# The first norm of a two-block transformer kernel: raw turn, normed tiles in PSUM, two units side by side

## The reference

```
h = x * rsqrt(mean(x * x, -1) + eps) * norm_mix          # x: 512 tokens x 1024
proj = h @ dn_w_in                                       # 1024 x (4 * 1024 + 16)
qkv = silu(depthwise_conv(proj[..., :3072], conv_w))     # 4 taps along the tokens
beta = sigmoid(b); g = -exp(a_log) * softplus(a + dt_bias)   # a, b: last 16 columns
k = l2_normalize(k)                                      # per head of 128
```

## Time and profile before

| | us |
|---|---|
| median of 3 runs | 1165.15 |
| lowest, highest | 1163.28, 1165.2 |
| the profiled execution | 1164.43 |
| its span (first to last instruction) | 1162.6 |
| TensorE busy | 1114.5 (96%) |
| TensorE weight loads | 908.2 (78%) |
| VectorE, GpSimd, ScalarE busy | 581.8, 486.7, 469.7 |

### The profile page before, as it was taken

One profiled execution on the slowest core, in us unless ns is written; L12 is line 12 of the kernel. 1 busy time (PEld: TensorE's weight loads), 2 busy tenths in 40 slices (PEclk: granted clock), 3 DMA queues, 4 the chain that ended last, 5 costly groups with the idle time before them and its releaser, 6 DMA issues. The chain is left out here.

```text
span 1162.6 us, 16417 instructions
## 1 busy us (share of the span) xinstructions
PE 1114.5 (96%) x5820; PEld 908.2 (78%) x5820; DVE 581.8 (50%) x1246; ACT 469.7 (40%) x1002; POOL 486.7 (42%) x280
## 2 busy tenths in 40 slices
PE   5999999999999899999999999899999999999995
PEld 4888888888887778888888888777788888656674
DVE  3576846666547564522122126445653654344465
ACT  5544345555534432431331333333333434343343
POOL 4575422323226584774674575454121211132220
PEclk8999999999999899999999999899999999999997
DMA  7453441221204453443443444422112010001001
GB/s 219 114 129 98 129 107 46 64 56 38 55 19 132 129 161 117 122 147 123 129 144 117 136 145 119 113 55 73 37 37 64 28 38 28 10 9 37 21 35 73
DMA packets 161175, 100.36 MB, mean 86 GB/s; under 512 B 24065, under 2 KB 154445, under 8 KB 160077
## 3 DMA queue, kind: packets, MB, share of 16 engines
q1 hardware_dynamic: 160812, 98.80, 29.5%
q10 hardware_dynamic: 288, 0.59, 0.2%
HBM read 96.21 MB, written 3.16 MB: 85 GB/s over the span
## 5 line engine op out<-in xcount | busy, mean ns | idle before, releaser
L1161 POOL TENSOR_TENSOR wlo<-stage,whi 128x1024 fp32r<-128x1024 f32 (+1 forms) x105 | 272.3, 2598 | 248.0 <-ACT whi L705 247.7
L2095 PE MATMUL ps<-hhi,whi 128*128 128x512 f32 (+1 forms) x744 | 307.3, 413 | 8.3 <-DVE hlo L1750 2.4
L2095 PE MATMUL ps<-hlo,whi 128*128 128x512 f32 (+1 forms) x744 | 303.0, 407 | 0.0
L2095 PE MATMUL ps<-hhi,wlo 128*128 128x512 f32 (+1 forms) x744 | 296.5, 398 | 0.0
L2095 PEld LDWEIGHTS ps<-hhi,whi 128*128 128x128 f32 (+1 forms) x744 | 141.9, 191 | 50.7 <-issue 17.1
L705 ACT ACTIVATE whi<-stage 128x1024 fp32r<-128x1024 f32 x104 | 109.5, 1055 | 130.3 <-PE ps L2095 99.6
L2095 PEld LDWEIGHTS ps<-hhi,wlo 128*128 128x128 f32 (+1 forms) x744 | 141.6, 190 | 25.6
L2095 PEld LDWEIGHTS ps<-hlo,whi 128*128 128x128 f32 (+1 forms) x744 | 142.0, 191 | 24.1 <-issue 2.8
L1250 POOL TENSOR_TENSOR wlo<-stage,whi 128x1024 fp32r<-128x1024 f32 (+3 forms) x40 | 73.4, 1838 | 197.7 <-ACT whi L991 197.7
L2095 PE MATMUL ps<-ahi,whi 128*128 128x512 f32 x320 | 127.7, 399 | 4.4 <-POOL alo L1238 2.8
L1067 ACT ACTIVATE prob<-ps,aneg 128x128 f32<-128x128 f32 (+1 forms) x96 | 50.6, 527 | 199.7 <-issue 102.1
(11 more groups left out here) (365 smaller groups left out, 1792.6 us busy)
## 6 DMA issues: line engine op xcount, KB each, us to landing
stage<-dn_w_in SPq DMA_DIRECT2D x32, 512.0 KB, 4.0
stage<-mlp_w_up SPq DMA_DIRECT2D x32, 512.0 KB, 4.5
stage<-mlp_w_down SPq DMA_DIRECT2D x32, 512.0 KB, 4.6
mod_w<-ada_w SPq DMA_DIRECT2D x8, 1536.0 KB, 6.4
stage<-w_in SPq DMA_DIRECT2D x17, 512.0 KB, 3.6
gcrow<-gc_rows SPq DMA_DIRECT2D x16, 256.0 KB, 3.5
stage<-dn_w_out SPq DMA_DIRECT2D x8, 512.0 KB, 3.6
stage<-w_in SPq DMA_DIRECT2D x9, 256.0 KB, 3.0
```

The costliest lines, as they stand in the source:

```text
L1161: pool.tensor_tensor(wlo[:, slot, 0:ks, 0:cols], stage[:, slot, 0:ks, 0:cols], whi[:, slot, 0:ks, 0:cols], ALU.subtract).then_inc(s["w_lo" ...
L2095: mm = pe.matmul(bank, w[:, slot, k - ks[0], 0:width], x[:, k], start=(i == 0), stop=(i == len(todo) - 1))
```

## The change

1. The first norm. x is transposed raw, a token tile at a time, as soon as it lands (`raw_turn(c)`, eight blocks into two banks), and VectorE copies it to `xT`. ScalarE still squares (now into `hlo` as waste) and takes roots, and then makes a diagonal matrix of the inverse roots (`root_diagonal`); a product of ones with it (`root_row`) lays the inverse roots as a row over all partitions in bank 7. `norm_mix` comes as 8 rows of 128 and is turned to a column per tile. VectorE makes each normed tile in one of five PSUM banks (`normed`), ScalarE copies its high part, VectorE subtracts the low part (`normed_low`). Nine products of the identity with itself, whose result is not used, follow the last root row.
2. Units 0 and 1 run side by side: for each tile as its `hhi` comes the high weights of both, and the low weights (those of unit 1 three tiles later); then the transposes of the vector rows; then all products with `hlo`, unit 1 four tiles behind.
3. ScalarE's first tap of `k0` and VectorE's three taps come ahead of the gates' last steps, ScalarE's tanh for `k0` ahead of the three exponentials, and the squares of `k0` ahead of the copy to `gct`. TensorE's sums for the gates stand after 15 products of `k1`, the transpose of `gcs` after 21. The raw transposes between products and their copies are gone.

The diff, cut to its core (left out: semaphore names, the tensors `diag`, `ones0`, `nmix`, `gcol`, which take the place of `gbc` and `xr`, and plain removals that the text above names):

```diff
+            def root_diagonal(c):
+                act.wait_ge(s["x_inv"], c + 1)
+                act.activation(diag[:, c, :], K["ident"], ACT.Copy, scale=rtok[:, 1, c:c + 1]).then_inc(s["x_dg"], 1)
+
+            act.wait_ge(s["ident_in"], 16)
             for c in range(CH):
                 act.wait_ge(x_in[c], 16)
-                act.activation(ps[:, 6:8, :], xn[:, c, :].rearrange("p (b n) -> p b n", b=2), ACT.Square,
+                act.activation(hlo[:, KT - 2:KT, :], xn[:, c, :].rearrange("p (b n) -> p b n", b=2), ACT.Square,
                                scale=float(D) ** -0.5, accum_out=msq[:, c:c + 1]).then_inc(s["x_sq"], 1)
                 act.wait_ge(s["x_sq"], c + 1)
                 act.activation(rtok[:, 0, c:c + 1], msq[:, c:c + 1], ACT.Sqrt, bias=epsc[:, :]).then_inc(s["x_rms"], 1)
-            for f in range(2 * CH):
-                c, half = f // 2, f % 2
-                act.wait_ge(s["h_tr"], f + 1)
-                act.activation(hhi[:, half * 4:half * 4 + 4, c * P:(c + 1) * P],
-                               ps[:, 2 + f % 4, :].rearrange("p (k i) -> p k i", k=4), ACT.Copy).then_inc(s["h_hi"], 1)
-            for n in range(1, 4):
+                if c:
+                    root_diagonal(c - 1)
+            root_diagonal(CH - 1)
+            split_hi(1, 1)
+            for k in range(KT):
+                act.wait_ge(s["x_f"], k + 1)
+                act.activation(hhi[:, k], hf0(k), ACT.Copy).then_inc(s["h_hi"], 1)
+            for n in range(2, 4):
                 split_hi(n, n)
...
 
             act.wait_ge(s["gate_in"], 32)
             act.activation(dtb[:, 1, :], dtb[:, 1, :], ACT.Exp).then_inc(s["gate_act"], 1)
+            act.wait_ge(s["vec_col"], 2)
+            tap0("k0")
             act.wait_ge(s["ba_col"], 1)
             act.activation(gtmp[:, 0], batok[:, :, 0:H], ACT.Tanh, scale=0.5).then_inc(s["gate_act"], 1)
             act.wait_ge(s["gate_dve"], 2)
@@ -766,25 +782,19 @@
             act.wait_ge(s["gate_act"], 3)
             act.activation(gtmp[:, 2], gtmp[:, 2], ACT.Ln, bias=1.0).then_inc(s["gate_act"], 1)
             split_hi(RING, 0)
-            act.wait_ge(s["vec_col"], 2)
-            tap0("k0")
+            conv_tanh("k0")
             act.wait_ge(s["gate_ps"], 1)
             for n in range(3):
                 act.activation(gates[:, :, 1 + n, :].rearrange("p h c -> p c h"),
                                ps[:, 4, 32 * n:32 * n + 32].rearrange("p (c h) -> p c h", h=H),
                                ACT.Exp).then_inc(s["gate_ready"], 1)
             act.activation(cact[:, :], V["c_2"], ACT.Tanh, scale=0.5).then_inc(s["mod_c"], 1)
-            conv_tanh("k0")
+            k_squares(0)
             act.wait_ge(s["gct_ps"], 1)
             act.activation(gct[0:H * CH, :], ps[0:H * CH, 4, P:2 * P], ACT.Copy).then_inc(s["gct_ready"], 1)
             next_split("k0")
...
+            pool.memset(ones0[:, :], 1.0).then_inc(s["ones_set"], 1)
...
+            dve.wait_ge(s["nm_tr"], 1)
+            dve.tensor_copy(gcol[:, :], ps[:, 0, 0:KT]).then_inc(s["nm_col"], 1)
+            for c in range(CH):
                 dve.wait_ge(s["x_rms"], c + 1)
                 dve.reciprocal(rtok[:, 1, c:c + 1], rtok[:, 0, c:c + 1]).then_inc(s["x_inv"], 1)
-                dve.wait_ge(s["x_inv"], c + 1)
-                dve.scalar_tensor_tensor(out=xr[:, c % 2], in0=xn[:, c, :], scalar=rtok[:, 1, c:c + 1], in1=gbc[:, :],
-                                         op0=ALU.mult, op1=ALU.mult).then_inc(s["x_nrm"], 1)
-
-            def h_low(f):
-                c, half = f // 2, f % 2
-                cut = (slice(0, P), slice(half * 4, half * 4 + 4), slice(c * P, (c + 1) * P))
-                dve.wait_ge(s["h_hi"], f + 1)
-                dve.tensor_tensor(hlo[cut], ps[:, 2 + f % 4, :].rearrange("p (k i) -> p k i", k=4), hhi[cut], ALU.subtract)\
-                    .then_inc(s["h_lo"], 1)
-
-            dve.wait_ge(s["gbc_in"], 16)
-            x_normed(0)
-            x_normed(1)
-            for c in range(CH):
-                for half in range(2):
-                    h_low(c * 2 + half)
-                if c < 2:
-                    x_normed(c + 2)
+                b = 2 + c % 2 * 2
+                dve.wait_ge(s["xtr"], c + 1)
+                dve.tensor_copy(xT[:, :, c * P:(c + 1) * P], ps[:, b:b + 2, :].rearrange("p b (k i) -> p (b k) i", k=KT // 2))\
+                    .then_inc(s["xev"], 1)
+            dve.wait_ge(s["nm_col"], 1)
+            dve.wait_ge(s["xev"], CH)
+            dve.wait_ge(s["rs_ps"], CH)
+
+            def normed(k):
+                if k >= 5:
+                    dve.wait_ge(s["h_lo"], k - 4)
+                dve.scalar_tensor_tensor(out=hf0(k), in0=xT[:, k], scalar=gcol[:, k:k + 1], in1=ps[:, 7, :],
+                                         op0=ALU.mult, op1=ALU.mult).then_inc(s["x_f"], 1)
+
+            def normed_low(k):
+                dve.wait_ge(s["h_hi"], k + 1)
+                dve.tensor_tensor(hlo[:, k], hf0(k), hhi[:, k], ALU.subtract).then_inc(s["h_lo"], 1)
+
+            for k in range(5):
+                normed(k)
+            for k in range(5, KT):
+                normed_low(k - 5)
+                normed(k)
+            for k in range(KT - 5, KT):
+                normed_low(k)
...
+            taps("k0")
...
+            silu2("k0", kT[:, 0])
...
+            pe.wait_ge(s["nm_in"], 16)
+            pe.transpose(ps[:, 0, 0:KT], nmix[0:KT, :], ident[0:KT, 0:KT]).then_inc(s["nm_tr"], 1)
+
+            def raw_turn(c):
+                pe.wait_ge(x_in[c], 16)
+                if c >= 2:
+                    pe.wait_ge(s["xev"], c - 1)
+                for k in range(KT):
+                    mm = pe.transpose(ps[:, 2 + c % 2 * 2 + k // 4, k % 4 * P:(k % 4 + 1) * P], xn[:, c, k * P:(k + 1) * P], ident)
                 mm.then_inc(s["xtr"], 1)
+
+            def root_row(c):
+                pe.wait_ge(s["x_dg"], c + 1)
+                pe.matmul(ps[:, 7, c * P:(c + 1) * P], ones0[:, :], diag[:, c, :], start=True, stop=True).then_inc(s["rs_ps"], 1)
+
+            pe.wait_ge(s["ones_set"], 1)
+            raw_turn(0)
+            for c in range(1, CH):
+                raw_turn(c)
+                root_row(c - 1)
+            root_row(CH - 1)
+            for _ in range(9):
+                pe.matmul(ps[:, 1, 0:P], ident, ident, start=True, stop=True)
 
             def some(stream, n):
                 for _ in range(n):
                     next(stream, None)
 
+            pe.wait_ge(s["ba_hi"], 1)
+            pe.wait_ge(s["w_hi"], 1)
+            first = ((0, BA_N, ps[0:BA_N, 0, :]), (1, P, ps[:, 1, :]))
+            for k in range(KT + 3):
+                for n, width, bank in first:
+                    if k < KT:
+                        if n == 0:
+                            pe.wait_ge(s["h_hi"], k + 1)
+                        pe.matmul(bank, whi[:, n, k, 0:width], hhi[:, k], start=(k == 0), stop=False)
+                for n, width, bank in first:
+                    x = k - n * 3
+                    if 0 <= x < KT:
+                        pe.wait_ge(s["w_lo"], n + 1)
+                        pe.matmul(bank, wlo[:, n, x, 0:width], hhi[:, x], start=False, stop=False)
             pe.wait_ge(s["vec_in"], 16 * (len(VEC_ROWS) + 4))
             pe.transpose(ps[:, 7, 0:NVEC], rows[0:NVEC, 0, :], ident[0:NVEC, 0:NVEC])
             pe.transpose(ps[:, 7, P:P + 96], rows[0:96, 1, :], ident[0:96, 0:96]).then_inc(s["vec_tr"], 1)
+            lag = 4
+            for k in range(KT + lag):
+                for n, width, bank in first:
+                    x = k - n * lag
+                    if 0 <= x < KT:
+                        if n == 0:
+                            pe.wait_ge(s["h_lo"], x + 1)
+                        mm = pe.matmul(bank, whi[:, n, x, 0:width], hlo[:, x], start=False, stop=(x == KT - 1))
+                        if x == KT - 1:
+                            mm.then_inc(s["w_used"], 1)
...
             stream = dn_unit("k1")
-            some(stream, 12)
+            some(stream, 15)
+            pe.wait_ge(s["const_in"], 16)
+            pe.wait_ge(s["gate_dve"], 4)
+            g2 = glog[:, :, :].rearrange("p c h -> p (c h)")
+            for n, m in enumerate(("upto", "after", "ones")):
+                mm = pe.matmul(ps[:, 4, 32 * n:32 * n + 32], K[m], g2, start=True, stop=True)
+            mm.then_inc(s["gate_ps"], 1)
+            some(stream, 6)
             pe.wait_ge(s["gcs_ready"], 1)
             pe.transpose(ps[0:H * CH, 4, P:2 * P], gcs[:, :, :].rearrange("p h c -> p (h c)"), ident).then_inc(s["gct_ps"], 1)
             some(stream, 24)
-            for k in range(4, KT):
-                raw_turn(k)
-            pe.wait_ge(s["xev_a"], 2)
             pe.wait_ge(s["gct_ready"], 1)
             k_products(0)
             for h in range(2, H):
```

More of the change, by code:

```diff
@@ L780, in _ @@
             next_split("k0")
-            k_squares(0)
             for h in range(1, H):
                 tap0(f"k{h}")
```

(33 more changed lines are left out.)

29 lines of the change are left out of this document (8 added, 21 removed).

## The result

The changed kernel took 1154.12 us (median of 4, 1153.53 to 1154.54), the kernel before beside it 1165.01 (4 runs, 1163.28 to 1165.2): ratio 0.9912 [0.9898, 0.9927], faster by 10.9 us. The profiled execution took 1153.77 us, span 1151.9; before 1164.43 and 1162.6. Forecast: 1155.2, a gain of 9.95.

The account below looks back on a forecast made before the run. TensorE was taken as the bound. `k2` starting 10.9 us earlier, less a new wait of 0.95 for the second squares, gave 9.95 us: 1155.2 from the median 1165.15, own range 1153.7 to 1156.8, 8 in 10 1152.5 to 1160.

Parts of the forecast that it names:

- S: Start of the first norm's normed tiles: 13.65 us, the middle of 12.9 (early clock) and 14.4 (all slow).
- The first pass: TensorE's 32 products with `hhi` for units 0 and 1: 7.3 us, paced by `hhi`, done at S+9.9.
- The gates: TensorE reaches the gates' sums about S+17.8 without a wait, then has a new wait of 1.0 us for `gcs`.
- The second squares: ScalarE's second key squares end at S+31.15, TensorE is there at S+30.2: a new wait of 0.95 us.
- Nothing further: Later key heads: GpSimd needs 5.4 us a head against TensorE's 7.3, so no more is lost.
- The cross-check: Second tally of the gain up to `k2`, from starts, raw transposes, clock and waits: 10.8 us, beside 10.9.
- The range: The forecast's own range, 1153.7 to 1156.8 us, from S of 12.9 to 14.4 and copy and PSUM prices.
- A: First norm: transposes don't raise the clock, first real product at 17.6; gain 8.0 us, time 1157.2; chance 0.15.
- B: TensorE's waits on GpSimd or transfers add 1 to 1.5 us at three places; 1158 to 1160; chance 0.13.
- C: Early clock, S = 12.9, no wait for `gcs` or the squares; gain 12.6 us, time 1152.6; chance 0.08.
- D: Clock stays low from the first product on, through gaps in TensorE's paced work; slower, to 1168; chance 0.03.
- E: Key heads give the head start back, GpSimd's order holding TensorE 1.4 us a head; 1163 to 1167; chance 0.03.

Follow-up runs that it names:

- the two repeats: The changed kernel, unedited, run twice more: 1154.55 and 1154.17 us, ratios 0.992 and 0.9912 to the kernel before.
- the last kernel: Changed kernel with gates' exponentials and `gcs` ahead of `k0`'s tanh and silu, and head 1's key squares ahead of the decay's exponential: 1151.55 us, ratio 0.9887.

## Why the prediction was right

The mechanism and the order of the chains were right: gain 10.9 us against 9.95. That the number is this close is partly luck, since the moment of the clock's rise alone moves it by 0.7, and the two repeats gained 9.6 and 10.4. Step by step:

- *S*, the term that was mis-sized: 12.69 measured, 13.65 taken. I took the middle between a clock that rises at 9 and one that never does; it rose at 8.7, and the tiles landed at 4.8, 6.1, 7.3 and 8.5 where 6.5, 7.8 and 9.0 were taken for the last three. Two prices beside it went the other way: a diagonal is 0.39, not 0.25, and the copy of 1024 is 1.23 (1.2 taken). In the repeats S was 12.87 and 13.40, so the bounds, 12.9 to 14.4, were nearly right and the low end the likelier.
- *First product* at S+1.53 (S+1.4 taken). *The first pass* ended at S+10.0 (S+9.9), the vector transposes and the `hlo` pass at S+14.17, where the small transposes begin (S+13.95). `normed` 0.75 with a pitch of 0.66, the low part 0.68: as priced. TensorE never waited for `wlo` there.
- *The gates*: sums at S+18.06 (S+17.8), the wait for `gcs` 0.96 (1.0). It ended at S+21.2, 0.4 later than taken: the silu took 1.03, and 0.68 or 0.69 for the next heads; a split on GpSimd ran beside it.
- *`k2`* starts at S+23.76 (S+23.65). *The second squares* end at S+30.96 (S+31.15), and the wait for them is 0.68 (0.95).
- *Nothing further*: right; from the third sums to the end the distance is that of before within 0.2 us.
- *The cross-check* has the 32 raw transposes at 3.8, the sum of their durations; by the distance between starts (35.69 to 37.43 for 16) they are 3.5. The main sum doesn't use this term. *The range*: S gives 0.75 either way, and the copy and PSUM prices that are to give as much again are not added up.

So of the sum, 0.96 came from S and 0.27 from the second wait, less 0.1 from S to `k2`: 11.1, of which 10.9 are seen at the third sums.

The rivals. *A* (transposes don't raise the clock) fell: in every profile of a raw turn the transposes' durations drop from 424 to about 274 ns between 8.3 and 11.3 us, with only transposes and at most a few small products of ones before it. In the kernel with 32 transposes back the rise at 8.3 has only transposes before it. The Trainium skill (TensorE: Matmul & The Clock Gate, Part 4) says that transposes don't raise the clock. These rows contradict it; the tile that it measured is bf16, these are fp32. *B* fell: no new wait of TensorE over 1 us appeared. *C* was half true, the early clock without the end of the waits; the last kernel shows its other half. *D* didn't occur here, but its mechanism is real and was priced too low as a danger: behind stalls of 1.90, 2.42 and 2.69 us in this region stood 3.3 to 6.7 us of low clock. *E* fell: from the third head on the sums of squares follow each other by 7.3 us in both kernels, so nothing is given back there.

What stays open: how much the removal of the broadcast and of the raw transposes is worth in the whole time. Their effects at the landmark, 0.8 to 1.0 and 1.4 us, were measured; in the medians they are within the scatter. And no kernel has the old norm with the rest of the change: of the 7.0 us at the first product the order of the units gives 2.6 (S+1.53 against S+4.12 with the units in turn), and that the rest comes from the first norm is read from the two timelines. What the runs do show is that a later S is carried on in full: from 12.69 to 13.88 the distance to the third sums stays 38.38 to 38.40.

## What to carry to other kernels

When a head start is gained on the bound engine, list the chains that did not shrink and compute when each ends from the same origin; those are the new waits, and here they were both named in advance and both removable by reordering ScalarE's and VectorE's queues (1.6 us at the landmark, 2.6 in the medians). An edit that moves one item on a queue moves whatever it feeds: the same reordering was a loss of 2.5 us in the median, by a low clock that seems to have come in three of its five runs, with one weight split moved along, and a gain of 0.9 without. At a stall like those of 1.90 to 2.69 us here, count the low clock that may follow: 3.3 to 6.7 us at half speed, which is up to half of that in time.

## What the runs showed of the hardware that I had not expected

- The rise of the clock under raw transposes came 3.3 to 6.0 us after the first one, at no fixed time: 8.7, 11.0 and 9.1 us in three profiles of the same kernel. S follows it (12.69, 13.40, 12.87).
- The clock fell in or right after waits of 2.69, 2.42 and 1.90 us, but not after 1.77 in the kernel without idle products; after 0.96 and 0.93 in the kernel with 18 idle products, but in no profile after 0.96 and 0.68. No run settles what tells these apart.
- The silu of 128x512 with two SBUF inputs takes 1.03 beside GpSimd's split and 0.78 in the last kernel, where about 0.2 of it ran beside that split; five low parts 5.28 instead of 3.08 when their input moved from PSUM to SBUF.
